# Layer norm over channels in a hybrid decoder step: from transposed tiles to channel-major sums

## The reference

```
c = conv(v) + b_dw                                   # causal depthwise convolution, 31 taps
xc = c - mean(c, channels)
c = silu(xc * rsqrt(mean(xc*xc, channels) + 1e-5) * ln_g + ln_b) * silu(z)
x1 = x + c @ w_out                                   # 1024 x 1024
h = rms_norm(x1)
k, v = split(h @ w_kv)                               # 512 columns, keys get a norm per head
q = h @ w_in_b[:, :1024]                             # 1024 columns, norm per head
```

## Time and profile before

| | |
|---|---|
| median of 3 runs | 1751.23 us |
| span of the profiled execution | 1746.1 us |
| busy: PE, DVE, ACT, POOL | 1683.0, 1280.0, 753.5, 588.1 us |
| granted TensorE clock over the span | 0.996 |

### The profile page before, as it was taken

How to read it: one execution, slowest core, us unless ns; L and a number is a source line. 1 busy time by engine, 2 the same in 40 slices (tenths; PEclk the granted TensorE clock), 3 DMA queues, 4 the chain that set the end, 5 groups by cost and what they waited for, 6 DMA issues and landing times.

```text
span 1746.1 us, 24190 instructions
## 1 busy us (share of the span) xinstructions
PE 1683.0 (96%) x8789; PEld 1377.8 (79%) x8789; DVE 1280.0 (73%) x2010; ACT 753.5 (43%) x1589; POOL 588.1 (34%) x433
## 2 busy tenths in 40 slices
PE   7999999999999979999999999979999999999999
PEld 6899888888899758888878888756777777777776
DVE  6379888999988558888778433567776777777774
ACT  6555556555536552323323232553333333333331
POOL 2489999999958003222333212100000000000000
PEclk9999999999999999999999999989999999999999
DMA  6311112111121754443554423644222323222221
GB/s 222 116 56 42 55 52 67 37 58 56 40 87 65 245 182 166 151 169 111 147 179 121 150 104 110 212 145 138 94 69 82 91 94 100 76 76 88 89 72 43
DMA packets 153849, 185.86 MB, mean 106 GB/s; under 512 B 51044, under 2 KB 116812, under 8 KB 149594
## 3 DMA queue, kind: packets, MB, share of 16 engines
q1 hardware_dynamic: 149418, 172.61, 30.9%
q10 hardware_dynamic: 4320, 11.80, 1.7%
HBM read 116.47 MB, written 70.72 MB: 107 GB/s over the span
## 4 chain that ended last, share of the span: by engine, by line
PE 58%; POOL 24%; DVE 7%; DMA 4%; issue 3%; ACT 3%; SPq 0%; POOLq 0%; DVEq 0%; ACTq 0%
POOL a_csum L488 21%; PE c_acc L121 18%; PE b_pso L121 12%; PE b_psq L121 8%; PE c_pso L2191 4%; PE c_pss L2168 3%; PE a_ps L740 3%; PE c_psp L2176 2%; DVE a_pst L638 2%; POOL a_csum L485 2%; DMA q_d<-b_qo 1%; PE c_pso L2185 1%; DVE b_x L1220 1%; PE c_pst L2097 1%; DVE w L109 1%
## 5 line engine op out<-in xcount | busy, mean ns | idle before, releaser
L740 PE MATMUL a_ps<-a_xt,a_wring 128*128 128x512 f32 (+3 forms) x2880 | 556.7, 354 | 9.0 <-ACT a_zo L550 5.8
L740 PEld LDWEIGHTS a_ps<-a_xt,a_wring 128*128 128x128 f32 x2880 | 494.2, 189 | 65.2 <-ACT a_zo L550 7.4
L488 POOL TENSOR_TENSOR a_csum<-a_prod,a_csum 128x704 f32<-128x704 f32 (+1 forms) x231 | 404.9, 1753 | 42.5 <-ACT a_prod L537 9.6
L638 DVE SCALAR_TENSOR_TENSOR a_pst<-a_vbuf,taps,a_pst 128x704 f32<-128x704 f32 (+1 forms) x338 | 314.1, 929 | 10.4
L537 ACT ACTIVATE a_prod<-a_vbuf,taps 128x704 f32<-128x704 f32 (+1 forms) x252 | 214.8, 863 | 165.7 <-POOL a_csum L488 154.1
L121 PE MATMUL c_acc<-w,c_ht 128*128 128x512 f32 x768 | 183.5, 395 | 1.3 <-issue 0.7
L121 PE MATMUL b_pso<-w,b_yt 128*128 128x512 f32 x768 | 179.1, 392 | 0.9 <-DVE b_yt L1209 0.9
L121 PEld LDWEIGHTS c_acc<-w,c_ht 128*128 128x128 f32 x768 | 141.7, 188 | 37.0 <-issue 8.4
L121 PEld LDWEIGHTS b_pso<-w,b_yt 128*128 128x128 f32 x768 | 142.8, 188 | 30.4 <-DVE b_yt L1209 1.4
L1727 ACT ACTIVATE c_es<-c_es 128x4 f32<-128x4 f32 x64 | 13.1, 205 | 232.7 <-DVE c_es L1882 232.7
L121 PE MATMUL b_pso<-w,b_ht 128*128 128x512 f32 x384 | 92.9, 398 | 10.1 <-DVE b_x L1220 5.9
(11 more groups left out here) (223 smaller groups left out, 2275.3 us busy)
## 6 DMA issues: line engine op xcount, KB each, us to landing
ht_d<-b_ht SPq DMA_DIRECT2D x16, 1024.0 KB, 3.9
c_ht<-ht_d SPq DMA_DIRECT2D x16, 1024.0 KB, 5.0
a_stage<-in_w_in_a SPq DMA_DIRECT2D x24, 512.0 KB, 4.0
a_x<-in_x_prompt SPq DMA_DIRECT2D x16, 512.0 KB, 3.9
b_cz<-c_d SPq DMA_DIRECT2D x16, 512.0 KB, 4.9
b_cz<-z_d SPq DMA_DIRECT2D x16, 512.0 KB, 6.1
b_x<-in_x_prompt SPq DMA_DIRECT2D x16, 512.0 KB, 3.5
x_d<-b_x SPq DMA_DIRECT2D x16, 512.0 KB, 3.0
```

Source lines behind the costliest of these rows:

```text
L488: pool.tensor_tensor(out, prod[:, (PTAPS * n + i) % RING, 0:t1 - t0], out, ALU.add).then_inc(prod_added, 1)
L638: dve.scalar_tensor_tensor(part if k == DTAPS - 1 and not last else here, vbuf[:, b % 2, t0 + k:t1 + k], wcol(k, b), part if k == 0 else h ...
L740: last = pe.matmul(out, wring[:, u % 3, a, k], xt[c][:, e, k, 0:n], start=(k == 0 and a == 0 and e == 0), stop=(k == KT - 1 and a == 1))
```

## The change

- Tiles 2 to 16 keep c channel-major. GpSimd adds the eight channel blocks of c to one in three adds of 512, 256 and 128 columns (`channel_sums`, into the buffer `qo`, here `part`). One matmul of TensorE with a matrix of 1/D gives each token's mean in all 128 partitions (`mean`). VectorE subtracts it from c into `yc` (`center`). ScalarE squares that into c's buffer (`square_c`), GpSimd adds the eight blocks again (`square_sums`), and one matmul gives the variance, a token a partition (`variance`). ScalarE adds eps, GpSimd makes the power (`deviation`), TensorE turns the result into a row in all partitions (`spread`), VectorE multiplies (`scale`). `silu_y` then reads `yc`. `bn_stats`, `turn_c` and `turn_y` go for these tiles; tiles 0 and 1 stay as they were.
- h is written over x instead of over y, except in tiles 0 and 16. So `scale_h` waits for the store of x1, and the next `load_x` for `turn_h`; in SyncE's `body` it now stands last. `load_c(t)` waits for a variance matmul instead of a transpose.
- `qkv` of tiles 1 to 15 does the first query half, then keys and values, then the second query half, with `spread(t+2)` and `mean(t+3)` between them. `out` begins with its second half from tile 2 on, so that the wait for the keys comes later.
- The orders of ScalarE and VectorE follow from this: `square_c` behind `cut_h`, `variance` behind the stores, `scale_h` ahead of `silu_y`, `center` behind `cut_h`, `scale` behind `residual` and two fills.

```diff
 def load_c(t):
-    after(sp, tc_done, t)
+    if t <= LEAST: after(sp, tc_done, t)
+    else: sp.wait_ge(var_mm, t - LEAST)
...
 # SyncE body, last line: load_x(t + 1), which waits for th_done
+def channel_sums(t):
+    pool.wait_ge(c_in, 16 * (t + 1))
+    pool.tensor_tensor(part[:, 0:4, 0:n], c[:, 0:4, 0:n], c[:, 4:8, 0:n], ALU.add).then_inc(sum_step, 1)
+    for k in (2, 1):
+        at += 1
+        pool.wait_ge(sum_step, at)
+        pool.tensor_tensor(part[:, 0:k, 0:n], part[:, 0:k, 0:n], part[:, k:2 * k, 0:n], ALU.add).then_inc(sum_step, 1)
+def square_sums(t):
+    pool.wait_ge(sq_ready, t - LEAST + 1)
+    for k in (4, 2, 1):
+        if k < 4: pool.wait_ge(sqsum_step, at)
+        pool.tensor_tensor(c[:, 0:k, 0:n], c[:, 0:k, 0:n], c[:, k:2 * k, 0:n], ALU.add).then_inc(sqsum_step, 1)
...
 # GpSimd body
-layer(t + 1)
+square_sums(t + 1)
+deviation(t + 1)
 power(g.rstd_b ...)
+channel_sums(t + 2)
 qk(t - 1)
...
 # VectorE body, t > 1
 cut_h(t - 1)
+center(t + 1)                 # yc = c - mean, waits mean_mm
 fill(begin)                   # odd t of 3 to 7
 queries(t - 2)
-normalize(t + 1, fill(3))
+fill(3)
 residual(t)
-fill(8)
+fill(4)
+scale(t + 1)                  # yc *= rstd, waits spread_mm and sq_ready
+fill(4)
 gate(t + 1, fill)
 keys(t - 1, lambda n: fill(4))
 fill(TAPS)
 query_sums(t - 1)
...
 # TensorE body
-turn_c(t + 1)
 out(t)                        # halves in the order 1, 0 from t = 2 on
-turn_y(t + 1)
+variance(t + 1)               # waits sqsum_step
-keys_values(); queries(0); queries(1)
+queries(0); spread(t + 1); keys_values(); mean(t + 2); queries(1)      # all of tile t - 1
 turn_h(t)
```

More of the change, by code:

```diff
@@ L1336, in body @@
                 if more:
-                    gate(t + 1, fill)
-            if not start:
-                if isinstance(t, int) and t == 1:
-                    split_weights_lo(dve, Q1, gains[Q1], w, 4)
-                keys(t - 1, lambda n: fill(4))
-                fill(TAPS)
-                if isinstance(t, int) and t == TILES:
-                    return
+                    center(t + 1)
+                if t not in (2, 4, 6, 8) and left is None:
+                    fill(begin)
+                queries(t - 2)
@@ new lines, in body @@
+            if left is not None or old is not None:
+                fill(3)
+            residual(t)
+            if t == 1:
+                split_weights_lo(dve, Q0, gains[Q0], w, 3, k0=KT // 2)
+            fill(4)
+            if more:
+                scale(t + 1)
+            fill(4)
+            if more:
+                gate(t + 1, fill)
+            if t == 1:
+                split_weights_lo(dve, Q1, gains[Q1], w, 4)
+            keys(t - 1, lambda n: fill(4))
+            fill(TAPS)
@@ L1422, in qkv, with queries @@
-            if between is not None:
-                between()
-            after(pe, q_ready, t)
-            if gate:
-                pe.wait_ge(ss_ready, 2)
-                pe.wait_ge(prev.z_copied, KT * NCH)
-            for b in range(2):
+            def queries(b):
+                if b == 0:
+                    after(pe, q_ready, t)
+                    if gate:
+                        pe.wait_ge(ss_ready, 2)
+                        pe.wait_ge(prev.z_copied, KT * NCH)
                 to = ps_q[:, b * HALF:(b + 1) * HALF]
@@ L1430, in qkv @@
                 ins = project(pe, to, ht, w.wslot[(Q0, Q1)[b]], n, (w.w_lo, KT * (3 + b)) if gate else None) if n == P else project_pair(pe, to, ht[:, 0], w.wslot[(Q0, Q1)[b]])
-                if late and b == 0:
-                    keys_values()
-            ins.then_inc(q_mm, 1)
+                if b == 1:
+                    ins.then_inc(q_mm, 1)
+            ahead = lambda: mean(t + 3) if t + 3 < ALL else None
+            back = lambda: spread(t + 2) if t + 2 < ALL else None
+            if gate or n == DEC:
+                keys_values()
+                if between is not None:
+                    between()
+                back()
+                queries(0)
+                ahead()
+                queries(1)
+            else:
+                queries(0)
+                back()
+                keys_values()
+                ahead()
+                queries(1)
```

199 lines of the change are left out of this document (127 added, 72 removed).

## The result

The changed kernel takes 1771.66 us in the median (1768.19 to 1775.98, 4 runs), the kernel before 1751.1 beside it: ratio 1.0124, 95% interval 1.0103 to 1.0145. It is slower by 1.2%, where 1754 was forecast and 1765 was the upper end of the range. The profiled execution took 1768.72 with a span of 1766.7, 20.6 more than the span before. A run's time lies only 1.8 (before) or 2.0 us (changed) above its span. So of the 5.1 us between the median before and the profiled span, some 3 are not "what lies around it" but the spread between executions; the changed kernel's profiled execution lies 2.9 under its median as well, so the two spans can be compared.

What follows compares the result with a forecast made beforehand. TensorE was taken to bound the kernel before, the new VectorE-ScalarE-GpSimd chain steps 2 to 7 of the changed one. +3.0 + 6.6 + 3.8 - 4.8 - 5.7 = +2.9 us on 1751.2 gave 1754.1, range 1739 to 1765.

Steps and rivals of the forecast that it cites:

- Steps 9 to 11: Phase B after step 8: TensorE bounds, c's sums are just in time for mean, 87.75 against 92.52 us, -4.8.
- steps 12 to 15: Late phase B, no taps: the chain is 5 us shorter than the step, 4 x -1.42 = -5.7 us.
- the three small pieces: TensorE's added variance, mean and spread: 0.95 us a step in all, set against 2.38 saved.
- Steps 0 and 1: +3.0: Start of phase B: late channel sums of tile 2 and weight pieces cost +3.0 us, ends 0 and +5.
- Steps 2 to 7: +6.6: Chain from one variance to the next, with tap and add collisions, bounds: 190.7 against 184.1 us.
- the clock is not in play: Kernel before, phase B steps 2 to 15: granted clock 1.00, the level of 2.4 GHz.
- V + 4.5 to 5: V is the start of variance in TensorE's queue; scale_h was to wait for x1's store until then, SiLU at 7.4.
- Step 8: +3.8: Late x and c: mean(10) and what follows in TensorE's queue wait 5.3 us; step 34.6 against 30.76.
- The rest, 0 forecast: Phase C starts on phase B's end and moves with it, with no change of its own.
- D: Rival: c's sums come too late for mean in steps 8 to 11, +15 us, 1766; chance 0.20.
- B: Rival: GpSimd's adds fit between the taps, steps 2 to 7 take 180.5, -12 us, 1739; chance 0.28.
- C: Rival: TensorE bounds in all steps, 14 x -1.42 = -20, 1734 us with the start; chance 0.07.

Runs made afterwards that it cites:

- e1: Changed kernel with 30 of the 31 taps of each old channel 8 columns wide instead of 704: 1740.09 us, ratio 0.9944.
- e5: Changed kernel with another order in steps 0 and 1 (mean(2), spread(2), scale(2), SiLUs, load_c(3) moved): 1761.91 us, ratio 1.0062.
- e4: Changed kernel with the key and value cache copies moved from steps 4 and 9 to 12 and 14: 1767.72 us, ratio 1.0115.
- e10: Changed kernel with the squares of x1 written over the low part of y, not the queries: 1771.77 us, ratio 1.0128.
- e2: Changed kernel with no taps between center and residual in steps 2 to 7; they run later in the step: 1763.95 us, ratio 1.0075.
- e6: Changed kernel with load_x ahead of store_old in steps 3, 5, 7 and no left part ahead of residual in step 8: 1770.27 us, ratio 1.0119.
- e9: e7 with queries ahead of the leftover taps, step 8's load_c(10) and first left part reordered, step 7's taps ended within it: 1744.86 us, ratio 0.9961.
- e12: e9 with the store of h ahead of the wait for the old channel, and step 8's last left part behind center of step 9: 1736.8 us, ratio 0.9928.
- e7: Changed kernel with leftover taps behind the next center, cache copies late, step 1 reordered and load_x ahead of the channel store: 1749.42 us, ratio 0.9993.

## Why the prediction was wrong

- **How much.** The span grew by 20.6 us where 2.9 was forecast. Of the 17.7 between them 6.7 lie in steps 0 and 1, 4.2 in steps 2 to 7, 1.9 in step 8, 3.3 in the rest and 2.0 ahead of the first projection; steps 9 to 15 came out 0.5 better.
- **Direction and mechanism were right.** TensorE's saving is eaten by the chain through center, squares, GpSimd, SiLU, gate and taps in steps 2 to 8 (e1). Steps 9 to 11 were -4.6 against -4.8 forecast, steps 12 to 15 were -6.4 against -5.7: a late step is 28.74, since the three small pieces cost less than the 0.95 I took for them (28.74 - 30.65 + 2.38, so some 0.5; three times 0.3 would have been 0.9).
- **The step that failed is above all "Steps 0 and 1: +3.0".** It measured +9.7. Counted from the first projection, the second tile's projection starts 4.3 us later than before (3.5 forecast), and by the first query half it is 3.7; that much is near the forecast. The second query half then starts 9.9 later. The 6.2 between these come with `mean(3)`, which the forecast put at nothing: it waits 8.71 us, because `load_c(3)` is issued only at 645.90, in SyncE's queue behind the load of z and weight pieces. Nor did I look at z, which holds ScalarE for 8.23 us. e5 gives back 10.8 of it in the profile and 9.8 in the median, by order alone.
- **"Steps 2 to 7: +6.6" measured +10.8.** Six intervals were forecast one by one and five of them are within 1.9. The one off is step 4's, 36.64 against 33.0, with the cache copy beside the stores that the chain waits for (e4, e10). The sign of it stood in the trace before. There, in step 9, the value cache's copy is issued at 872.77, and the squares wait for the query store behind it:

```profile
876.60 0.34 ACTq L1118 DMA_DIRECT2D q_d<-b_qo  x1
885.18 1.06 ACT L1070 ACTIVATE b_qo<-b_x 128x1024 f32<-128x1024 f32 x1 [12.31 <-DMA q_d<-b_qo]
```

  The store took 8.6 us, the step 31.02 and not 30.7: the kernel before had no chain that could feel more of it. I wrote that h over x makes `scale_h` wait until V + 4.5 to 5 "ahead of SiLU at 7.4", at the median landing, and never asked for the worst.
- **The clock.** I wrote that "the clock is not in play". In the changed kernel it is. The granted clock of steps 2 to 7 is 0.97 (1.00 before), and single windows of it behind waits of 1.53, 5.78 and 3.50 us are these:

```profile
742.35:748.15 5.80, 5.80 (x26) 4.78 (x27) 2.58 (x3) 0.26 (x1) 1.18 (x1) 1.00 0.77 287
779.44:786.24 6.80, 6.80 (x26) 5.46 (x26) 2.13 (x3) 2.45 (x4) 2.49 (x4) 0.80 0.49 157
843.94:850.92 6.98, 6.98 (x27) 5.59 (x27) 2.15 (x3) 2.45 (x4) 3.21 (x4) 0.78 0.51 150
```

  0.80 and 0.78 mean that part of the window ran at 1.2 GHz, the rest at 2.4. Twenty-four products then take 6.97 and 7.14 us, not 5.7: a wait of 3.5 us costs 4.9. In steps 0 to 8 of the changed kernel it happened six times, for 1.3 to 2.7 us each (618.73, 634.95, 657.04, 779.44, 843.94, 891.70). Not all of it is new. The kernel before has the one at 634.95 too:

```profile
629.24 7.33 PE L121 MATMUL b_pso<-w,b_ht 128*128 128x512 f32 x24 [3.89 <-issue]
```

  And the second query half of step 1 takes 8.36 us at half clock where it took 8.8 before, with waits for its weights. The other four are new, 5.5 of the 26 us lost in steps 0 to 8. The Trainium skill, TensorE: Matmul & The Clock Gate, section "What's actually happening", says that the gate has two states and falls to half when the engine has been idle. The rows agree on both; which waits bring the fall they show only case by case (behind 1.80 us in e2 it fell, behind 2.77 in the changed kernel it did not). The forecast had a wait of 5.3 us in step 8 without a clock price on it.
- **Step 8: +3.8** measured +5.75. The wait of `mean(10)` is there, 4.23 against 5.3; e6 confirms the place. Beside it stand the half clock behind it (1.45 us) and waits of 0.85 before `variance` and 0.25 for the residual, which the forecast put at nothing.
- **The rest, 0 forecast, measured +3.3.** At phase C's start a load of keys and values keeps TensorE waiting 0.89 instead of 0.19, and the next 16 query products take 5.53 instead of 3.9, at a clock of 0.68. This is 2.3 of it; why the load lands later was not tried and stays open.
- **The rivals.** D came near the time, 1766, but not where it was put: in steps 9 to 11 `mean` waits once, 1.28 us. Sums of c that come too late did cost time, in step 1, where D did not look. B is refuted by the adds' means, C by e1: only without the taps does TensorE bound steps 2 to 8.

## What to carry to other kernels

When work moves from an engine that is full to a chain over three that are not, price the chain by its worst transfer, not the median one, and list every wait of each engine's queue that now stands inside it, in the first steps as well as in the steady ones. The waits of TensorE of 3.5 to 5.8 us in steps 5, 7 and 8 cost their length and about 1.4 us more each. Of a version that loses, look for order first: without a change to the arithmetic this one went from 1.2% slower to 0.7% faster by moving instructions, loads and stores in the queues.

## What the runs showed of the hardware

- Transfers issued together delayed one another: x1's store of 512 KB, 3.0 us in the median, took 6.8 us beside four others (e9) and 4.5 with the 1 MB store of h taken out of the group (e12); c's load took 8.1 and 5.8.
- GpSimd's adds and VectorE's multiply-adds excluded one another (e2), but GpSimd's power did not. In e7 two taps with two SBUF inputs take 1.93 us, 0.97 each as when alone, and the first lies wholly beside the power:

```profile
718.37 2.92 POOL L1025 TENSOR_TENSOR b_hrs<-b_hms,minus_half 128x16 f32<-128x16 f32 x1
720.17 1.93 DVE L1374 SCALAR_TENSOR_TENSOR b_conv<-b_three,taps,b_conv 128x704 f32<-128x704 f32 x2
```
